# Differential attention: both score sets of a head in one slot, the second in other banks, two heads one and two slots later

## The reference

```python
q1, q2 = qh[..., 0, :], qh[..., 1, :]      # 4 heads, two halves of 128, q scaled by 128 ** -0.5
k1, k2 = kh[..., 0, :], kh[..., 1, :]
def probs(qq, kk):
    s = einsum('bhqd,bhkd->bhqk', qq, kk) + bias
    return softmax(where(mask, s, -inf))
a = probs(q1, k1) - lam * probs(q2, k2)
o = einsum('bhqk,bhkd->bhqd', a, v)        # v: 256 wide
o = rmsnorm(o, g_head, 1e-5) * (1 - lambda_init)
```

## Time and profile before

| | before |
|---|---|
| median of 3 runs | 2977.11 us (2976.90 to 2977.66) |
| the profiled execution | 2976.74 us, span of its trace 2975.0 us |
| PE busy | 2961.7 us of the span |
| DVE busy | 2261.4 us |
| ACT busy | 1467.9 us |
| POOL busy | 58.1 us |
| DMA | 283.30 MB, 95 GB/s in the mean |
| mean granted clock of TensorE | 0.999 |

### The profile page before, as it was taken

The page is one execution under the profiler, slowest core; times in us unless marked ns, Lnnn a source line. Parts: engine busy times, 40 slices in busy tenths (PEclk is TensorE's granted clock), DMA queues, the critical chain, the costliest instruction groups (busy, mean ns, idle before and its releaser), DMA issues.

```text
span 2975.0 us, 48001 instructions
## 1 busy us (share of the span) xinstructions
PE 2961.7 (100%) x18781; PEld 2655.5 (89%) x18781; DVE 2261.4 (76%) x2787; ACT 1467.9 (49%) x2155; POOL 58.1 (2%) x148
## 2 busy tenths in 40 slices
PE   9999999999999999999999999999999999999999
PEld 8779999888889999878899998888999878899998
DVE  7978888576759887566598875658888567588984
ACT  4476555454345555444455553325555354355554
POOL 6100000000000000000000000000000000000000
PEclk9999999999999999999999999999999999999999
DMA  6122332342133332311333333223333222133322
GB/s 189 49 72 92 101 125 93 111 137 71 56 101 99 99 105 100 94 64 56 105 101 99 99 107 105 87 68 115 102 100 106 92 85 66 62 114 99 106 99 78
DMA packets 256759, 283.30 MB, mean 95 GB/s; under 512 B 11938, under 2 KB 229216, under 8 KB 256616
## 3 DMA queue, kind: packets, MB, share of 16 engines
q1 hardware_dynamic: 256504, 281.28, 29.1%
q10 hardware_dynamic: 112, 0.02, 0.0%
HBM read 279.16 MB, written 4.73 MB: 95 GB/s over the span
## 4 chain that ended last, share of the span: by engine, by line
PE 89%; DVE 6%; ACT 2%; issue 1%; POOL 1%; DMA 1%; DVEq 0%; SPq 0%; ACTq 0%; POOLq 0%
PE ps L2946 39%; PE ps L2571 13%; PE ps L2573 13%; PE ps L2572 13%; PE ps L3303 1%; PE ps L3304 1%; PE ps L3305 1%; PE ps L3210 1%; PE ps L3270 1%; PE ps L3249 1%; PE ps L3289 1%; PE ps L3291 1%; PE ps L3290 1%; PE ps L3159 1%; PE ps L3140 0%
## 5 line engine op out<-in xcount | busy, mean ns | idle before, releaser
L840 ACT ACTIVATE whi<-raw 128x2048 fp32r<-128x2048 f32 (+2 forms) x144 | 246.6, 1712 | 467.8 <-PE ps L2573 386.7
L1519 DVE TENSOR_TENSOR wlo<-raw,whi 128x2048 fp32r<-128x2048 f32 (+2 forms) x144 | 293.6, 2039 | 219.5 <-ACT whi L840 219.2
L2946 PE MATMUL ps<-th,wh 128*128 128x256 f32 x1600 | 453.7, 284 | 0.6 <-DVE wl L1608 0.5
L2946 PE MATMUL ps<-tl,wh 128*128 128x256 f32 x1600 | 452.7, 283 | 0.0
L2946 PE MATMUL ps<-th,wl 128*128 128x256 f32 x1600 | 452.7, 283 | 0.0
L2571 PE MATMUL ps<-hh,whi 128*128 128x512 f32 x896 | 357.4, 399 | 0.0
L2573 PE MATMUL ps<-hh,wlo 128*128 128x512 f32 x896 | 349.7, 390 | 0.0
L2572 PE MATMUL ps<-hl,whi 128*128 128x512 f32 x896 | 349.4, 390 | 0.0
L2946 PE MATMUL ps<-hh,wh 128*128 128x256 f32 x1200 | 340.1, 283 | 0.2
L2946 PE MATMUL ps<-hh,wl 128*128 128x256 f32 x1200 | 339.6, 283 | 0.0
L2946 PE MATMUL ps<-hl,wh 128*128 128x256 f32 x1200 | 339.6, 283 | 0.0
(11 more groups left out here) (524 smaller groups left out, 6693.1 us busy)
## 6 DMA issues: line engine op xcount, KB each, us to landing
raw<-in_w_ffn_in SPq DMA_DIRECT2D x88, 1024.0 KB, 5.1
raw<-in_w_in SPq DMA_DIRECT2D x59, 1024.0 KB, 5.2
raw<-in_w_ffn_out SPq DMA_DIRECT2D x40, 1024.0 KB, 5.0
raw<-in_w_o SPq DMA_DIRECT2D x32, 640.0 KB, 4.0
raw<-in_w_gate SPq DMA_DIRECT2D x11, 1024.0 KB, 5.3
raw<-in_w_up SPq DMA_DIRECT2D x11, 1024.0 KB, 5.3
raw<-in_w_down SPq DMA_DIRECT2D x10, 1024.0 KB, 5.0
raw<-in_w_out SPq DMA_DIRECT2D x4, 1024.0 KB, 5.3
```

Source lines behind the costliest of these rows:

```text
L840: a.activation(whi[:, slot, 0:n], raw[:, slot, 0:n], ACT.Copy).then_inc(hi_made, 1)
L1519: v.tensor_tensor(wlo[:, u % 2, 0:n], raw[:, u % 2, 0:n], whi[:, u % 2, 0:n].bitcast(F32), ALU.subtract).then_inc(lo_made, 1)
L2946: e = mm(bank(b, HALF), wgt[:, q, w], xx, start=start and k == 0 and m == 0, stop=k == KD // 2 - 1 and m == 2, skip_group_check=True)
```

## The change

`DZ` goes from [20, 28, 36, 48] to [20, 29, 38, 48]. A table `DQ` gives each score set its own columns of PSUM: the first keeps `ZQ`, the second lies in banks 6 (columns 3072 and 3200), 7 (3584) and 3 (1536), where the values' products and the sum of squares of the head also go. PE issues both sets in slot DZ. The second no longer waits for `d_s`; for head 0 it waits for `d_lamexp`, for the others until the head before has been normalised (`d_on`) and its root is taken (`d_sd`). On DVE and ACT the steps of a set stay at their distances from DZ. As 28 and 36 are no longer in `DZ`, `scores_first` holds for units 5 and 12 only.

```diff
-DZ = [20, 28, 36, 48]
+DZ = [20, 29, 38, 48]
+
+DQ = (ZQ, {0: 3072, 2: 3200, 3: 3584, 1: 1536})
...
-                            v.tensor_tensor(dp[c][:, ZQ[i]:ZQ[i] + wq(i)], ps[:, ZQ[i]:ZQ[i] + wq(i)],
+                            v.tensor_tensor(dp[c][:, ZQ[i]:ZQ[i] + wq(i)], ps[:, DQ[c][i]:DQ[c][i] + wq(i)],
                                             dbias[:, T - wq(i):T], ALU.add).then_inc(S("d_s"), 1)
...
-                for c in range(2):
-                    for hd in at_slot(DZ, s, c):
-                        m = 2 * hd + c
-                        if c:
-                            pe.wait_ge(S("d_s"), 4 * m)
+                for hd in at_slot(DZ, s):
+                    for c in range(2):
+                        if c and hd:
+                            pe.wait_ge(S("d_on"), 2 * hd)
+                            pe.wait_ge(S("d_sd"), hd)
+                        elif c:
+                            pe.wait_ge(S("d_lamexp"), 1)
                         elif hd:
                             pe.wait_ge(S("d_pt"), hd)
                         else:
                             pe.wait_ge(mix_ready, m0 + 2)
                         pe.wait_ge(acc_free, g0 + evicted(unit_of(hd, 1), c))
                         for i in (0, 2, 3, 1):
-                            e = mm(ps[:, ZQ[i]:ZQ[i] + wq(i)], qp[hd % 2][:, c, P * i:P * i + P], kp[hd % 2][:, c, 0:wq(i)],
+                            e = mm(ps[:, DQ[c][i]:DQ[c][i] + wq(i)], qp[hd % 2][:, c, P * i:P * i + P], kp[hd % 2][:, c, 0:wq(i)],
                                    start=i != 2, stop=True, skip_group_check=True)
                         e.then_inc(S("d_z"), 1)
```

## The result

The changed kernel takes 2988.45 us in the median of 7 runs (2987.03 to 2989.49), the kernel before 2976.94 in the median of 7 (2976.65 to 2977.66): 11.5 us slower, ratio 1.0038 with a 95% interval of 1.0028 to 1.0047. The profiled execution took 2989.49 us, with a span of 2987.8; it is the slowest of the seven.

What follows compares the result with a forecast made beforehand. TensorE, busy 2961.7 of 2975.0 us, was taken to bound the kernel. New waits of 8.67 us, less 0.51 and 0.16, give +8.0; with 1.4 for the clock, 2977.1 becomes 2986.5 us, range 2983.8 to 2989.4.

Steps and rivals of the forecast that it cites:

- case A: The forecast itself, chance 0.45: all waits as summed and the clock falls in the long one, 2986.5 us.
- E: Rival, chance 0.10: 2 to 5 us above the sum, from a longer clock fall or head 2's chain; 2990 us.
- slot 20, less its merge: Head 0's second set waits 0.15 us for lambda's exponential; merging two sets saves 0.04 us a head.
- slot 29: Head 1's second score set waits 1.0 us for head 0's normalisation, which DVE does after a weight split.
- transposes, slot 34: Head 1's transposes wait 2.25 us (1 to 3), as a split stands between DVE's two probability steps.
- clock after slot 34: Behind the wait of head 1's transposes no fall of the clock was counted: 0.
- sum of squares, slot 36: Head 1's sum of squares waits 5.17 us for DVE's addition, behind both halves of a weight split.
- clock after slot 36: Price of a clock fall in the long wait for head 1's squares: 1.4 us, between 0 and 3.3.
- head 2's transposes: After the split and both probability steps on DVE, head 2's transposes wait 0.1 us (0 to 1).
- PE's own work: Two score sets together cost 7.08 us in place of 7.12, saving 0.16 in all; the bank costs nothing.
- a fall during the wait is likely: In slot 36 the clock was expected to drop during the 5.2 us wait, 3.2 us into it.
- Rival B: Chance 0.32: the same waits as in the forecast, but the clock stays up; 2985.1 us.

Runs made afterwards that it cites:

- e8: The changed kernel with banks and slots kept and only the orders of steps on DVE and ACT mended; 2976.04 us, against 2976.90 before the change.
- e9: The changed kernel with head 1's bias on DVE put behind head 0's normalisation in slot 28; 2986.64 us.
- e1: The changed kernel with DVE's addition of head 1's squares put ahead of the weight split that opens unit 9; 2983.03 us.
- e6: The kernel before with only the slots moved to 20, 29, 38, 48, old banks and waits kept; 2988.31 us.
- e2: The changed kernel with the weight split that opens unit 7 put behind slot 28 on DVE; 2988.90 us.
- e3: The changed kernel with the weight split that opens unit 8 put behind slot 32 on DVE; 2985.59 us.
- e10: The changed kernel with only the wait before slot 34's transposes filled with 9 matmuls that nothing reads; 2987.41 us.
- e5: The changed kernel with the old slots 20, 28, 36, 48, so only the banks and the shared slot are new; 2991.16 us.
- e7: The changed kernel with slots 20, 30, 39, 48; 2979.77 us.

## Why the prediction was right, point by point

The range held the time (2983.8 to 2989.4; 2988.45) and the sign was right. The mechanism was that of case A, all waits and a fall in the long one, but 2.0 us above its 2986.5: the time lies between A and E (2990), and more came from the clock, as E had said, though from a second fall and not a longer one. Term by term, from the profile of the changed kernel (the slowest of its seven executions, 1.0 us above the median):

| term | forecast | measured |
|---|---|---|
| slot 20, less its merge | 0.1 | 1307.71 - 1289.52 - 18.02 = 0.2 |
| slot 29 | 1.0 | 1344.77 - 1324.98 - 17.96 = 1.8 |
| transposes, slot 34 | 2.25 | 1346.99 - 1344.77 = 2.2 |
| clock after slot 34 | 0 | 1352.48 - 1346.99 - 3.90 = 1.6 |
| sum of squares, slot 36 | 5.17 | 1364.76 - 1359.57 = 5.2 |
| clock after slot 36 | 1.4 | 1373.03 - 1364.76 - 6.60 = 1.7 |
| head 2's transposes | 0.1 | 0.1 |

(18.02 and 3.90 are the same stretches in the kernel before; 17.96, 6.60 and the ends of the slots 33 and 35, 1344.77 and 1359.57, are worked out from its durations and the last matmul before the wait, as the prediction did. Unrounded the terms sum to 12.7; less the 0.5 that the transposes waited before and 0.1 for the merges of heads 1 and 2 that is the 12.1 of the profile.)

**PE's own work.** Right: a block of both sets takes as long as the values of a head, and e8 shows the gain of the merge where nothing else is left.

**Slot 20.** Right in kind and size.

**Slot 29.** The term that was mis-sized: 1.8 us, not 1.0. The step "DVE does the split at the start of slot 28 and the normalisation after it" left out head 1's bias. With DZ[1] = 29 it stands in slot 28, ahead of the normalisation; the prediction counted it for head 2 and forgot it here. e9 shows its 0.7 us.

**Slot 34.** Right to 0.1 us. The bias left out in slot 29 makes both sides of this wait later alike, as DVE's chain starts from PE's slot 29; e9, where PE comes 0.7 us sooner and the wait stays at 2.1, shows it.

**Slot 36.** Right, and the reading by the order of the queues is what e1 and e6 confirm.

**The clock.** The step that failed is "a fall during the wait is likely" with one wait in mind: the fall behind the wait of 2.2 us was put at nothing, and it came in this profile, at 1.6 us, and in two of five others. It is the largest term that the sum lacks. Rival B, in which the clock stays up, falls: all eight waits of 5.0 us in the profiles had a fall. The 1.4 us for it came out near the 1.6 of this profile by luck in part. The prediction had the fall 3.2 us into the wait and 2.0 of the slow stretch inside it; here the clock fell 0.2 us after the wait's end and stayed down for 3.4 us. In the eight waits it fell 3.1 to 5.4 us after the wait began. The price follows how long it stayed down: 1.6 to 1.7 us in six falls of 3.4 us, from 0.3 us before a wait's end to 1.3 after it, and 2.5 to 2.8 in five of 6.8 us, which began 0.7 to 1.9 us before the end (e2, e3, e10, the second ones of e5 and e6). The bound of 3.3 held for each single fall. The Trainium skill (TensorE: Matmul & The Clock Gate, Part 1) says that a quiet engine falls back to half rate; the granted clock of 0.50 between 1365 and 1368 agrees.

**Missed in the estimate of what is late next.** After a wait was taken away, the next one was where the expectation put it in e2 and not in e1, e7 and e9. Each time an eviction on DVE that itself waits for PE had been left out of the chain, in e7 besides that ACT's order of split and exponentials had been taken the wrong way round.

## What to carry to other kernels

A step that is moved to another slot moves past all that stands at the start of that slot on its engine. Before moving, write down for each engine what opens the slot; if that waits for the engine which in turn waits for the moved step, the whole round trip (here 5.2 us: ACT's half, DVE's half, the addition) is laid bare, however idle the engines are. When a gain is under a microsecond, as here (0.7 us in e8's profile), such a round trip outweighs it several times, and the same move with six steps put in a better order costs nothing.

## What the runs showed of the hardware

A wait of TensorE can cost more than its length. Behind three of six waits of 2.1 to 3.0 us, and towards the end of all eight of 5.0 (from 1.9 us before it to 0.2 after), the granted clock went to 0.50 (1.2 GHz), and it came back after 3.4 or 6.8 us. A fall of 3.4 us cost 1.6 to 1.7 us, one of 6.8 us, which began 0.7 to 1.9 us before the wait's end, 2.5 to 2.8. Work that nobody reads, put into the wait, gave this back (2.3 us in the median for two waits). None of the nine waits of 1.4 to 1.7 us in the layer (slot 29 in six profiles, e1's 1.4 in slot 36, e7's 1.7 and 1.4) had a fall behind it.
